# Trainium2 trunk step: window attention moved from a stage of its own into the delta-rule steps

## The chip, the cores and the metric

The kernel runs on one core of one Trainium2 chip. The metric is the device time of one execution in microseconds. A core has engines with instruction queues of their own: TensorE (PE, its weight loads shown as PEld), VectorE (DVE), ScalarE (ACT), GpSimd (POOL) and SyncE (SP), which here issues all transfers. They wait for one another by semaphores.

## The reference, cut to what matters

Two layers are run over 128 prompt tokens and 512 sample tokens. The change concerns the mixer of the even layer, which has two halves side by side behind one input projection:

```
qa, ka, va, qkv_b, gate_b, ab = split(h @ w_in)
# half A: softmax attention, 8 heads of 64, 2 key heads, a sink logit for each head
prompt: oa = softmax_sink(qa ka^T / 8) va                      # 128 queries, 128 keys
sample: qa, ka = rope(qa), rope(ka)
        for each of 4 tiles of 128 queries: keys = 128 cached + the tile and its two neighbours, |q - k| <= 128
# half B: gated delta rule, 4 heads of 128, forwards and backwards over the tiles, a state carried along
for each chunk: A = strict(K K^T * decay * beta);  R = (I + A)^-1
        v_new = R (beta v - beta decay K S);  o = (q decay) S + (QK^T * decay) v_new;  S = decay S + K^T v_new
ob = rmsnorm(o_fwd + o_bwd, out_norm) * silu(gate_b)
out = concat(oa, ob) @ w_out
```

The adaLN modulation of both layers, silu(c) @ w_mod, reads a matrix of 1024 x 12288 floats and is needed in pieces from the even layer's output on.

## The kernel before, in words

Activations lie with features on partitions and 640 token columns (TW) side by side: tile 0 is the prompt, tiles 1 to 4 the sample. Matrix products with large weights are made from three products of rounded halves (hi and lo): `hi` on ACT makes the high part, `w_rest` on DVE the low one. Everything runs in the order in which each engine's part of the program is written; nothing is scheduled at run time.

The even layer has these stages. First the input projection, 23 blocks of 128 columns (`proj`); the last four of them, E_GATE and on, are the gate blocks, and keys and values of half B are turned to token rows between them (`kv_turn`, copied out of PSUM by `k_rows` on ACT and on DVE). Then five delta steps, `for r in range(NT)`: step r handles one tile in each direction (c = 0 forwards, c = 1 backwards; the fifth handles the prompt both ways). In a step the triangular inverse is built in levels: at each level PE makes a product into the z part of a bank (`crossed_mm`, L2418), DVE masks it (`level_z`, L1705), PE makes two products of it (L2471, L2474), and DVE adds them (`r_blocks`, `t_blocks`, L1711, L1714). After the levels come the solve (L2528), the decay rows of the next step (`gc_rows`, L2372) and output and state (L2542, L2543, L2545).

In the gaps of each step PE makes 8 pieces of the modulation product, each with 1 MB of w_mod (`mod_piece`, `mod_first_half`, L2212, L2221). SP loads the pieces two halves ahead into MSLOTS = 4 buffers, a buffer being free when `mod_done` says that its piece is used. Each step also rotates one block of queries or keys of half A (`rope_swap_a`, L2364, and three DVE operations).

After the delta steps comes the attention stage: 40 units (tile, head) in the order of ALLU. For a unit PE makes scores (`att_scores`, L2577, two heads in one call), DVE adds the mask and takes the row maximum (L1806), ACT takes the exponential with its sum (L1095) and that of the sink (L1097), PE turns the probabilities (`att_turn`, L2202), ACT copies them (L500), PE multiplies with the values (`att_values`, L2600), and DVE scales by the reciprocal sum (L1791). The norm and gate of half B (`on_step`) are spread over the same units, and `keep_busy` products (L2207) stand between them. Then `out_halves(0)` begins the output projection (L2081) with blocks m = 0 and 1, and ACT's `out_proj(0)` splits the weights from m = 2 on (L1115).

Of the kernel before, what the change touches and what calls it, by code (L numbers as in the profile page):

```python
# [109 lines left out]
def build(nc, a, outs):  # L110
# [21 lines left out]
    NORMS = (("first", KD, 1), ("l2", 8, 8), ("on", 4, 8), ("cq", C_Q // P, 1), ("ckv", C_KV // P, 1))  # L132
# [162 lines left out]
    MSLOTS = 4  # L295
# [3 lines left out]
    MROW = place("mod_rows", [512], R_T + 4 * al(TW))  # L299
    SM = [place(f"scores{s}", [512], R_F + 1024 + 512 * s) for s in range(2)]  # L300
    PR = [place(f"probs{s}", [512], R_F + 2048 + 512 * s) for s in range(2)]
    PT = [place(f"probs_t{s}", [512], R_F + 3072 + 512 * s) for s in range(2)]
    ASM = place("attn_small", [256], R_F + 4096)
    OA = [place(f"o_attn{s}", [512], R_F + 512 * s) for s in range(2)]
# [154 lines left out]
    ALLU = [(t, c + 4 * g2) for t in ATT for c in range(4) for g2 in range(2)]  # L459
    A_ROPE = (4, 0, 1, 2, 3)  # L460
    ON_AT = [4 + 8 * h for h in range(B_HEADS)]

    def on_head(u, step):

        return ON_AT.index(u - step) if u - step in ON_AT else None

# [25 lines left out]

    def att_copy_a(act, u):

        t, h = ALLU[u]
        c0, c1 = att_local(t)
        act.wait_ge(S("a_turned"), u + 1)
        if u >= 2:
            act.wait_ge(S("a_pv"), u - 1)
        act.activation(PT[u % 2][:, c0:c1], PS[:, 1024 + 512 * (u % 2) + c0:1024 + 512 * (u % 2) + c1], ACT.Copy  # L500
                       ).then_inc(S("a_pt"), 1)


# [60 lines left out]
    with stack:  # L564
# [4 lines left out]
        def _(sp):  # L569
# [43 lines left out]
            for n in range(23):  # L613
                if n < E_AB:
                    load(n, ein_v[:, :, (6 + n) * P:(7 + n) * P])
                elif n == E_AB:
                    load(n, ein_v[:, :, 22 * P:22 * P + 16])
                    sp.dma_start(CT[:, C_FOUR, 0:16], consts[:, C_FOUR, 0:16]).then_inc(S("consts_landed"), 16)
# [3 lines left out]
                elif n < E_QA + 4:  # L622
                    load_two(n, [ein_v[:, :, 64 * h:64 * h + 64] for h in (n - E_QA, n - E_QA + 4)])
                else:
                    c = n - E_QA if n < E_GATE else n - 1
                    load(n, ein_v[:, :, c * P:(c + 1) * P])
            sp.dma_start(CT[:, C_AMASK:, :], consts[:, C_AMASK:, :]).then_inc(S("consts_landed"), 16)
# [130 lines left out]
        def _(act):  # L758
# [238 lines left out]

            for r in range(NT):
                for c in range(2):
# [6 lines left out]
                    act.activation(DQ[c][:, :, :], DQ[c][:, :, :], ACT.Exp, scale=-1.0).then_inc(S("d_exp"), 1)  # L1006
                for c in range(2):
# [43 lines left out]
            o_copy(NT - 1, 0)  # L1051


            def on_step(u):

                h = on_head(u, 0)
                if h is not None:
                    if h == 0:
                        for c in range(2):
                            act.wait_ge(*both("o_done", c, NT))  # L1060
                    if h >= 2:
                        act.wait_ge(*of("stat", "on", 2 * (h - 1)))
                    act.activation(ONSQ[h % 2][:, :], OD[:, h, :], ACT.Square).then_inc(S("norm_sq"), 1)
                for hf in range(2):
                    cs = slice(hf * HW, hf * HW + HW)
                    h = on_head(u, 2 + 2 * hf)
# [21 lines left out]
            for u, (t, h) in enumerate(ALLU):  # L1088
# [10 lines left out]
                if u >= 1:  # L1099
                    att_copy_a(act, u - 1)  # L1100
# [1734 lines left out]
```

## Time and profile before

| what | value |
|---|---|
| runs | 1902.68 us median of 3 (1900.95 to 1903.35) |
| the profiled execution | 1901.23 us, of which the span from first to last instruction is 1899.4 us |
| PE, PEld busy | 1808.8 us (95%), 1667.0 us (88%) |
| DVE, ACT, POOL busy | 988.6, 816.0, 55.8 us |
| TensorE clock granted, mean | 0.997 of full speed |
| the five delta steps | 221.5 to 434.2 us of the span |
| the attention stage | 434.2 to 529.6 us |

A matmul's busy time counts from its start to its modelled end, so a row of n matmuls is shorter than n times their mean: they overlap. A float matrix product in 32 bits stands in the trace as two records, a turn by transposition as one.

### The profile page before, as it was taken

The page shows a single profiled execution, that of the slowest core. Times are in us where ns is not written, and L with a number is a line of the kernel's source. Part 1 is how long each engine was busy: PE and PEld are TensorE (multiplying, and loading weights), DVE is VectorE, ACT ScalarE, POOL GpSimd, SP SyncE. Part 2 cuts the span into 40 slices and gives each one's busy share as a digit, 9 for nine tenths or more (in the row PEclk, how much of TensorE's full clock was granted, in tenths as well). Part 3 has the DMA queues.
Part 4 walks back from the last instruction along what each step waited for, and adds up shares of the span by engine and source line. Part 5 has one row for each costly group of instructions (what it writes and reads, how often), then busy time and mean ns, then how long its engine had stood idle before and what let it go on. Part 6 is the DMA issues. An engine that isn't in the chain of part 4 may idle for free. (4 is left out here: it accounts for less than half of the span.)

```text
span 1899.4 us, 36570 instructions
## 1 busy us (share of the span) xinstructions
PE 1808.8 (95%) x14803; PEld 1667.0 (88%) x14803; DVE 988.6 (52%) x1838; ACT 816.0 (43%) x1396; POOL 55.8 (3%) x57
## 2 busy tenths in 40 slices
PE   5999989988899999999999999999999999999998
PEld 3999867667799999999999887776899999999997
DVE  4443345656747655235556843344376553355555
ACT  4545422225745544124445654343455442243453
POOL 0000222220000000000000000000000000000000
PEclk9999999999999999999999999999999999999999
DMA  7232376751021222222234311011211232122243
GB/s 289 67 69 57 122 222 214 214 178 57 1 72 45 78 74 86 72 67 74 70 99 140 94 49 31 24 33 31 67 45 56 77 89 78 56 77 77 81 135 117
DMA packets 244627, 170.25 MB, mean 90 GB/s; under 512 B 20922, under 2 KB 231068, under 8 KB 243356
## 3 DMA queue, kind: packets, MB, share of 16 engines
q1 hardware_dynamic: 244508, 168.55, 29.8%
q8 instruction: 88, 1.44, 0.3%
q14 instruction: 31, 0.25, 0.0%
HBM read 165.09 MB, written 3.44 MB: 89 GB/s over the span
## 5 line engine op out<-in xcount | busy, mean ns | idle before, releaser
L769 ACT ACTIVATE w_hi<-w_raw 128x1024 fp32r<-128x1024 f32 (+4 forms) x186 | 197.7, 1063 | 529.2 <-PE ps L2003 416.1
L1351 DVE TENSOR_TENSOR w_lo<-w_raw,w_hi 128x1024 fp32r<-128x1024 f32 (+4 forms) x190 | 233.0, 1227 | 346.9 <-ACT w_hi L769 346.5
L2003 PE MATMUL ps<-h_hi,w_hi 128*128 128x320 f32 x1632 | 373.9, 310 | 4.4 <-ACT conv L1178 2.4
L2003 PE MATMUL ps<-h_hi,w_lo 128*128 128x320 f32 x1632 | 371.8, 309 | 0.0
L2003 PE MATMUL ps<-h_lo,w_hi 128*128 128x320 f32 x1632 | 371.7, 309 | 0.0
L2003 PEld LDWEIGHTS ps<-h_hi,w_hi 128*128 128x128 f32 x1632 | 272.8, 188 | 6.5 <-ACT conv L1178 2.9
L2003 PEld LDWEIGHTS ps<-h_lo,w_hi 128*128 128x128 f32 x1632 | 273.0, 188 | 0.0
L2003 PEld LDWEIGHTS ps<-h_hi,w_lo 128*128 128x128 f32 x1632 | 272.8, 188 | 0.0
L2081 PE MATMUL ps<-g_hi,w_hi 128*128 128x320 f32 x352 | 110.1, 313 | 3.2 <-DVE g_lo L1850 2.0
L2081 PE MATMUL ps<-g_lo,w_hi 128*128 128x320 f32 x352 | 108.8, 309 | 0.0
L2081 PE MATMUL ps<-g_hi,w_lo 128*128 128x320 f32 x352 | 108.8, 309 | 0.0
L1357 DVE SCALAR_TENSOR_TENSOR conv<-u,vec_cols,conv 128x511 f32<-128x511 f32 x200 | 101.3, 548 | 14.4 <-ACT conv L1178 11.6
L1361 DVE SCALAR_TENSOR_TENSOR conv<-u,vec_cols,conv 128x511 f32<-128x511 f32 x200 | 100.7, 546 | 0.0
L2081 PE MATMUL ps<-h_hi,w_out_hi 128*128 128x320 f32 x288 | 90.4, 314 | 0.1
L2081 PE MATMUL ps<-h_hi,w_out_lo 128*128 128x320 f32 x288 | 89.0, 309 | 0.0
L2081 PE MATMUL ps<-h_lo,w_out_hi 128*128 128x320 f32 x288 | 89.0, 309 | 0.0
L1183 ACT ACTIVATE g_hi<-gated 128x640 f32 (+1 forms) x44 | 32.6, 742 | 105.1 <-DVE gated L1848 105.1
L2081 PEld LDWEIGHTS ps<-g_hi,w_hi 128*128 128x128 f32 x352 | 66.1, 188 | 4.5 <-DVE g_lo L1850 2.5
L1178 ACT ACTIVATE conv<-ps,vec_cols 128x640 f32<-128x640 f32 x88 | 69.3, 787 | 0.0
L2081 PEld LDWEIGHTS ps<-g_lo,w_hi 128*128 128x128 f32 x352 | 66.1, 188 | 0.2
L2081 PEld LDWEIGHTS ps<-g_hi,w_lo 128*128 128x128 f32 x352 | 66.1, 188 | 0.0
L1868 DVE COPY f_t<-ps 128x640 f32 (+1 forms) x16 | 13.2, 825 | 98.3 <-PE ps L2003 80.5
(364 smaller groups left out, 3299.6 us busy)
## 6 DMA issues: line engine op xcount, KB each, us to landing
w_raw<-in_ffn_w_up SPq DMA_DIRECT2D x88, 512.0 KB, 3.8
w_mod_raw<-in_w_mod SPq DMA_DIRECT2D x80, 512.0 KB, 4.5
w_raw<-in_ffn_w_down SPq DMA_DIRECT2D x48, 704.0 KB, 4.6
w_raw<-in_ev_w_in SPq DMA_DIRECT2D x18, 512.0 KB, 3.8
w_mod_first<-in_w_mod SPq DMA_DIRECT2D x8, 1024.0 KB, 15.8
w_raw<-in_ev_w_out SPq DMA_DIRECT2D x8, 512.0 KB, 4.7
w_raw<-in_od_w_out SPq DMA_DIRECT2D x8, 512.0 KB, 4.1
w_raw<-in_od_w_kv_up SPq DMA_DIRECT2D x24, 128.0 KB, 2.3
```

Source lines behind the costliest of these rows:

```text
L769: act.activation(WH[slot][:, 0:k, :], RAW[slot][:, 0:k, :], ACT.Copy).then_inc(w_hi, 1)
L1178: act.activation(halves(Y[b][:, :]), pair(b0 + 2 * slot), ACT.Copy, scale=vcol(v0 + b * FCH, j)).then_inc(evac_a, 1)
L1183: act.activation(row(Gh, j), GP[:, :], ACT.Copy).then_inc(S("g_hi_written"), 1)
L1351: dve.tensor_tensor(WL[slot][:, 0:k, :], RAW[slot][:, 0:k, :], WH[slot][:, 0:k, :].bitcast(F32), ALU.subtract).then_inc(w_lo, 1)
L1357: dve.scalar_tensor_tensor(y[:, c0 + 1:c1], u[:, c0:c1 - 1], w_before, y[:, c0 + 1:c1], ALU.mult, ALU.add).then_inc(S(signal), 1)
L1361: dve.scalar_tensor_tensor(y[:, c0:c1 - 1], u[:, c0 + 1:c1], w_after, y[:, c0:c1 - 1], ALU.mult, ALU.add).then_inc(S(signal), 1)
L1868: dve.tensor_copy(halves(row(F, m)), pair(2 * slot)).then_inc(evac_v, 1)
L2003: last = pe.matmul(out, w_of(k, wi), x_of(k, xi, i), start=(k == 0 and p == 0), stop=(k == ks - 1 and p == 2))
L2081: last = pe.matmul(out, w[wi][:, k, :], x[xi][:, k, tk(g)], start=(k == 0 and p == 0), stop=(k == ks - 1 and p == 2))
```

## The change

- The attention stage goes. Step r of the delta loop now carries all heads of one tile (r = 0 the prompt, r = 1 to 4 the sample tiles 1 to 4). The two heads c and c + 4, which have different key heads, form a pair. Scores of pair q are made at level q (0 to 3), its maxima on DVE at level q + 1, its two turns at level q + 2 and its values at level q + 3, the last of them in the final level. The scores lie in banks 2 and 5, the values in the upper half of banks 1 and 4, and the products of the levels move to the banks that are left.
- In the prompt's step all eight heads are one batch: scores at level 1, maxima at level 2, turns at levels 3 and 4, values at level 5.
- The sink's exponential and the division are made once a step for eight heads (`sink_args`, `att_sink`, `normalise`); the result is turned at the start of the next step and copied into the place of the queries.
- The rope products go to the gate blocks (E_GATE - 1 to 22), one after each, on bank 7, so `kv_turn` has three banks (4, 5, 6) in turn where it had four.
- MSLOTS falls from 4 to 3; the tables for mask, cosine and sine are loaded earlier.
- Within a step k_times_state moves from levels 4 and 5 to levels 0 and 1, and piece 6 of the modulation from level 5 to the final one.
- Norm and gate of half B and the split of half A follow as a tail (`on_square` ... `on_rest`), 640 columns at a time; `first_chunks` multiplies each 128 rows of the activations with output blocks 0 and 1 as they come. The `keep_busy` products of this place go.

```diff
-    MSLOTS = 4
+    MSLOTS = 3
-    A_ROPE = (4, 0, 1, 2, 3)
+    A_ROPE = (0, 1, 2, 3, 4)
+    S_BANK, O_BANK, O_AT = (2, 5), (1, 4), 128
+    TAIL = (0, 1, 2, 4, 3, 5, 6, 7)
@@ ScalarE
-                act.activation(KTOK[:, t, :, :], q4(bank(4 + 2 * (t % 2))), ACT.Copy).then_inc(S("k_tok"), 1)
+                act.activation(KTOK[:, t, :, :], q4(bank(4 + (2 * t) % 3)), ACT.Copy).then_inc(S("k_tok"), 1)
...
+                att_exps(r, 0)
+                for q in range(pairs(r)):
+                    att_pt_copy(r, q, 0)
+                    if q + 1 < pairs(r):
+                        att_exps(r, q + 1)
+                    else:
+                        att_sink(r)
+                    att_pt_copy(r, q, 1)
...
-            for u, (t, h) in enumerate(ALLU):
...
+            on_square(0)
+            att_hi(0)
+            hi(N0_EVEN_OUT)
+            on_square(1)
+            on_root(0)
...
+            on_out(3)
-            act.wait_ge(S("on_lo"), B_HEADS)
+            act.wait_ge(S("on_lo"), 4 + B_HEADS)
             out_proj(0)
@@ VectorE, after the masks level_z of a level
+                    if r == 0:
+                        if lv == 1:
+                            sink_scaled()
+                        elif lv == 2:
+                            prompt_max()
+                        elif lv == 3:
+                            sink_args(0)
+                    elif lv < 5:
+                        pair_max(r, lv - 1)
+                    else:
+                        sink_args(r)
...
+                normalise(r)
                 for c in range(2):
                     dve.wait_ge(*both("v_solved", c, r + 1))
@@ TensorE
             def kv_turn(t):
-                for kind, sem in ((1, "k_tok"), (2, "v_tok")):
-                    if t >= 2:
-                        pe.wait_ge(S(sem), t - 1)
+                for kind in (1, 2):
+                    x = 2 * t + kind - 1
+                    if x >= 3:
+                        pe.wait_ge(S(("v_tok", "k_tok")[kind - 1]), (x - 3) // 2 + 1)
...
+                if n >= E_GATE - 1:
+                    rope_swap_a(n - E_GATE + 1)
...
+                if r > 0:
+                    att_out_turn(r - 1)
...
+                        if lv < 4:
+                            mod_first_half(r, lv + 2)
+                        if lv == 1 and r < NT - 1:
+                            k_times_state(r, 1)
+                        if lv > 2:
+                            for c in range(2):
+                                pe.wait_ge(*both("t_written", c, t0 + lv))
+                            att_values(r, lv - 3)
+                        if lv > 1:
+                            att_turn(r, lv - 2, 0)
...
+                        if lv < 4:
+                            mod_piece(r, lv + 2, halved=True)
+                        if lv > 1:
+                            att_turn(r, lv - 2, 1)
+                        if lv < 4:
+                            att_scores(r, lv)
...
                 if r < NT - 1:
+                    pe.wait_ge(S("oa_scaled"), r + 1)
                     gc_rows(r + 1)
...
-            pe.wait_ge(S("a_rotated"), NT)
-            keep_busy(7, 3)
...
+            att_out_turn(NT - 1)
+            mod_turn(MROUNDS + 1, MROW, 6)
...
+            out_halves(0, on_stat)
```

On TensorE, the third step's (r = 2) level 3 before: the two products of z, half a piece of the modulation, the product for level 3 of both directions, the other half (names as in the code; the rows of 64 x 32 products repeat).

```order
L2418 MATMUL ps<-r_blocks_176,a_blocks_178 64x64 x8
L2418 MATMUL ps<-r_blocks_177,a_blocks_179 64x64 x8
L2221 MATMUL ps<-w_mod_raw_190,silu_c 32x256 x4
L2471 MATMUL ps<-level_z_170,t_blocks_172 64x32 x2
L2474 MATMUL ps<-t_blocks_172,level_z_170 64x32 x2
...
L2221 MATMUL ps<-w_mod_raw_190,silu_c 32x256 x4
```

The same place now:

```order
L2589 MATMUL ps<-r_blocks_176,a_blocks_178 64x64 x8
L2589 MATMUL ps<-r_blocks_177,a_blocks_179 64x64 x8
L2330 MATMUL ps<-w_mod_raw_189,silu_c 32x256 x4
L2547 MATMUL ps<-v_attn_tok,probs_t 128x64 x8
L2311 MATMUL ps<-consts,probs_193 128x128 x4
L2660 MATMUL ps<-level_z_170,t_blocks_172 64x32 x2
L2663 MATMUL ps<-t_blocks_172,level_z_170 64x32 x2
...
L2330 MATMUL ps<-w_mod_raw_189,silu_c 32x256 x4
L2311 MATMUL ps<-consts,probs_193 128x128 x4
L2517 MATMUL ps<-qa_ka_va 128x128 x4
L2517 MATMUL ps<-k_ctx_cols,qa_ka_va 128x128 x2
L2517 MATMUL ps<-qa_ka_va 128x128 x2
```

The values of pair 0 and the first turn of pair 1 stand between the z products and the level's own, and the second turn and the scores of pair 3 behind them.

On VectorE, level 2 of the same step now; before, the two masks were followed at once by the four additions.

```order
L1813 TENSOR_TENSOR level_z_170<-ps,consts 128x256
L1813 TENSOR_TENSOR level_z_171<-ps,consts 128x256
L1739 ISA probs_193,attn_small<-ps,consts,sink_scaled 128x512
L1739 ISA attn_small 128x1
L1739 ISA probs_193,attn_small<-ps,consts,sink_scaled 128x512
L1739 ISA attn_small 128x1
L1713 TENSOR_SCALAR attn_small<-attn_small 128x2
L1833 TENSOR_TENSOR r_blocks_176<-r_blocks_176,ps 128x32x4
L1836 TENSOR_TENSOR t_blocks_172<-t_blocks_172,ps 128x32x4
L1833 TENSOR_TENSOR r_blocks_177<-r_blocks_177,ps 128x32x4
L1836 TENSOR_TENSOR t_blocks_173<-t_blocks_173,ps 128x32x4
```

The mask and maximum of a pair stand between the masks of z and the additions that wait for the level's products.

On ScalarE, the head of the tail, behind the last copy of the delta output; before, these stood among the exponentials of the units.

```order
L1001 ACTIVATE qa_ka_va<-ps 128x4x128
L1107 ACTIVATE on_sq_205<-o_delta 128x640
L1112 ACTIVATE h_hi<-qa_ka_va 128x640
L769 ACTIVATE w_hi_58<-w_raw_56 128x1024
L1107 ACTIVATE on_sq_206<-o_delta 128x640
L1119 ACTIVATE on_rstd_207<-ps,eps 128x640
L1122 ACTIVATE on_rstd_207<-on_rstd_207 128x640
L769 ACTIVATE w_hi_57<-w_raw_55 128x1024
```

They are whole rows of 640 columns in a fixed order, 20 of them and two weight blocks.

## Rows read from the trace of the kernel before

**Rows 1.** Windows by stage: length, busy of each engine, clock, DMA share, GB/s.

```profile
219.40:270.00 50.60, 43.14 (x819) 32.87 (x819) 24.35 (x70) 15.03 (x34) 11.85 (x12) 0.93 0.73 223
315.00:357.00 42.00, 38.75 (x811) 29.73 (x811) 25.75 (x79) 11.68 (x30) 10.91 (x10) 1.00 0.67 207
436.00:482.00 46.00, 40.19 (x355) 33.26 (x355) 31.40 (x124) 32.36 (x89) 0.00 (x0) 1.00 0.10 30
```

**Rows 2.** Timeline of DVE: each step's first operation, and the last state.

```profile
221.51 1.49 DVE L1672 TENSOR_TENSOR d_qk<-ps,decay_sum 128x512 f32<-128x512 f32 x2 [8.41 <-PE ps L2372]
...
268.39 0.69 DVE L1672 TENSOR_TENSOR d_qk<-ps,decay_sum 128x512 f32<-128x512 f32 x1 [3.64 <-PE ps L2545]
...
312.87 0.69 DVE L1672 TENSOR_TENSOR d_qk<-ps,decay_sum 128x512 f32<-128x512 f32 x1 [2.45 <-PE ps L2545]
...
352.33 0.69 DVE L1672 TENSOR_TENSOR d_qk<-ps,decay_sum 128x512 f32<-128x512 f32 x1 [2.45 <-PE ps L2545]
...
395.29 0.69 DVE L1672 TENSOR_TENSOR d_qk<-ps,decay_sum 128x512 f32<-128x512 f32 x1 [2.45 <-PE ps L2545]
...
434.44 0.69 DVE L1748 COPY state<-ps 128x512 f32<-128x512 f32 x1 [1.04 <-PE ps L2545]
```

**Rows 3.** Timeline of one pair: scores, next work, a turn, values, mask and exponential.

```profile
456.27 0.75 DVE L1806 CUSTOM_DVE_ANT_0 scores<-ps,consts,sink_scaled 128x512 f32<-128x512 f32 x1
457.29 0.71 ACT L1095 ACTIVATE probs<-scores,attn_small 128x512 f32<-128x512 f32 x1
457.84 0.71 PE L2577 MATMUL ps<-qa_ka_va 64*128 64x128 f32 x8
458.93 0.66 PE L2202 MATMUL ps<-consts,probs 128*128 128x128 f32 x4
459.31 0.97 PEld L2600 LDWEIGHTS ps<-v_attn_tok,probs_t 128*128 128x128 f32 x8
```

**Rows 4.** Groups of the window 315:357: count, busy, mean, idle before and releasers.

```profile
L2471 PEld LDWEIGHTS ps<-level_z,t_blocks 64*64 64x64 f32 x160 | 5.1, 134 | 1.5 <-DVE level_z L1705 1.2
L2418 PEld LDWEIGHTS ps<-r_blocks,a_blocks 64*64 64x64 f32 x160 | 5.1, 134 | 2.3 <-DVE r_blocks L1711 1.2 <-issue 0.8 <-DVE r_blocks L1699 0.2
...
L2510 PEld LDWEIGHTS ps<-level_z,t_blocks 64*64 64x64 f32 x16 | 0.6, 134 | 1.3 <-DVE level_z L1732 1.3
```

**Rows 5.** Windows of 3 us after a wait for w_mod, as in rows 1.

```profile
237.00:240.00 3.00, 0.35 (x4) 0.23 (x8) 0.36 (x1) 0.00 (x0) 0.00 (x0) 0.77 0.47 156
240.00:243.00 3.00, 3.00 (x80) 2.00 (x72) 0.82 (x4) 0.00 (x0) 0.00 (x0) 0.50 0.75 221
243.00:246.00 3.00, 3.00 (x48) 1.94 (x40) 1.00 (x3) 0.00 (x0) 0.00 (x0) 0.59 0.81 264
```

**Rows 6.** Timeline of PE: a wait inside one group of products.

```profile
284.99 0.24 PE L2471 MATMUL ps<-level_z,t_blocks 64*64 64x32 f32 x1 [2.15 <-issue]
```

**Rows 7.** Transfers of w_mod in 318:335, from issue to landing.

```profile
DMA to landing us min/median/max: 3.9/4.4/5.0
```

**Rows 8.** Timeline after the first gate block: turns on PE, then ACT.

```profile
193.76 1.91 PE L2202 MATMUL ps<-consts,qkv_b 128*128 128x128 f32 x16
...
197.01 1.08 ACT L945 ACTIVATE k_tok<-ps 128x512 f32<-128x512 f32 x2
```

**Rows 9.** Groups of 433:530 that the tail keeps, as in rows 4.

```profile
L1063 ACT ACTIVATE on_sq<-o_delta 128x640 f32<-128x640 f32 x4 | 2.9, 723 | 0.0
L769 ACT ACTIVATE w_hi<-w_raw 128x1024 fp32r<-128x1024 f32 x2 | 2.1, 1046 | 0.0
L1763 DVE TENSOR_TENSOR o_delta<-o_delta,silu_gate 128x640 f32<-128x640 f32 x4 | 3.3, 818 | 0.0
```

**Rows 10.** Timeline: table load and weights on ACT and DVE, first product of block m = 2.

```profile
528.78 1.28 ACT L1126 ACT_TABLE_LOAD   x1
...
531.17 2.36 DVE L1464 TENSOR_TENSOR w_out_lo<-w_raw,w_out_hi 128x1024 fp32r<-128x1024 f32 x2 [1.68 <-ACT w_out_hi L1115]
...
536.70 0.31 PE L2081 MATMUL ps<-h_hi,w_out_hi 128*128 128x320 f32 x1
```

More of the change, by code:

```diff
@@ L298, in build @@
     MPARTS = KD * MROUNDS
[L299 to L304, printed above, removed]
+    MROW = place("mod_rows", [512], R_G + 5 * TW)
+    SM = [place(f"probs{s}", [2, 512], R_RAW + MSLOTS * 2 * D + 1024 * s) for s in range(2)]
+    ASM = place("attn_small", [256], R_RAW + MSLOTS * 2 * D + 2048)
+    assert MSLOTS * 2 * D + 2304 <= 6 * KMAX * P
+    PT = place("probs_t", [2, 512], R_T + 2176)
+    OA = place("o_attn", [512], R_A + (NT + 3) * P + 16)
     KW = PAST + TW
@@ new lines, in on_out @@
+            def on_out(h):
+                act.wait_ge(S("on_gated"), 2 * h + 2)
+                act.activation(Hh[:, 4 + h, :], OD[:, h, :], ACT.Copy).then_inc(S("on_hi"), 1)
+            for c in range(2):
+                act.wait_ge(*both("os_done", c, NT))
+            on_square(0)
[3 more added lines that the diff above has]
+            on_root(0)
+            hi(N0_EVEN_OUT + 1)
+            att_hi(1)
+            on_square(2)
+            on_root(1)
+            att_hi(2)
@@ L1111, in out_split @@
+            on_square(3)
+            on_out(0)
+            att_hi(3)
+            on_root(2)
+            on_out(1)
+            on_root(3)
+            on_out(2)
+            on_out(3)
             def out_split(n0, m):
@@ L1773, in rope @@
+            mod_out(MROUNDS - 1, 6)
+            att_lo(0)
+            w_rest(N0_EVEN_OUT)
+            on_gate(0)
+            w_rest(N0_EVEN_OUT + 1)
+            att_lo(1)
+            att_lo(2)
+            on_gate(1)
+            on_rest(0)
+            att_lo(3)
+            on_gate(2)
+            on_rest(1)
+            on_gate(3)
+            on_rest(2)
+            on_rest(3)
+            for i in range(4, 8):
+                gains(i // 4, i // 2 % 2, 1 + i % 2)
             def rope(dst, b, turned, n):
@@ new lines, in att_turn @@
+            def att_turn(r, q, g2):
+                p = batch(r, q)
+                pe.wait_ge(S("a_exp"), p + 1)
+                if q or g2:
+                    pe.wait_ge(S("a_pt"), 2 * p + g2)
+                elif r == 0:
+                    pe.wait_ge(S("k_out_rows"), 1)
+                elif r < NT - 1:
+                    pe.wait_ge(*both("v_minus", 1, r + 1))
+                else:
+                    pe.wait_ge(S("mod_cols"), r + 1)
+                for c0 in [P * c for c in range(4)] if r == 0 else [c0 for c0, kt in att_tiles(r)]:
+                    last = turn(PS[:, 7 * 512 + c0:7 * 512 + c0 + P], SM[p % 2][:, g2, c0:c0 + P])
+                last.then_inc(S("a_turned"), 1)
@@ new lines, in att_values @@
+            def att_values(r, q):
+                p = batch(r, q)
+                pe.wait_ge(S("a_pt"), 2 * p + 2)
+                if r == 0:
+                    pe.wait_ge(S("v_rows"), 2)
+                for c in range(4) if r == 0 else (q,):
+                    for g2 in range(2):
+                        o0 = 512 * O_BANK[g2] + O_AT + 64 * c
+                        tiles = [(P * c, 0)] if r == 0 else att_tiles(r)
+                        for x, (c0, kt) in enumerate(tiles):
+                            last = pe.matmul(PS[:, o0:o0 + 64], PT[:, g2, c0:c0 + P], AV[:, kt, 64 * g2:64 * g2 + 64],
+                                             start=(x == 0), stop=(x == len(tiles) - 1))
+                last.then_inc(S("a_pv"), 1)
@@ L2389, in _, with att_out_turn @@
+            def att_out_turn(t):
+                pe.wait_ge(S("oa_scaled"), t + 1)
+                for k in range(4):
+                    last = turn(hb(7, k), OA[:, P * k:P * k + P])
+                last.then_inc(S("oa_turned"), 1)
             gc_rows(0)
```

551 lines of the change are left out of this document (265 added, 286 removed).

## Prediction

> **What bounds the kernel now.** I read the windows by stage first, to see which engine fills which stage. In the delta steps [rows 1] PE is busy 43.14 of 50.6 us in the first step and 38.75 of 42 in the third, while DVE has 24 to 26 us and ACT 12 to 15; the transfers of w_mod move 207 to 223 GB/s. In the first half of the attention stage PE shows 40.19 of 46 us, but there dummy products are counted, and DVE (31.40) and ACT (32.36) work on small pieces. Nobody is full there: the stage is a round of short waits between three engines. It lasts from 434.2 (last product of state; the copy of it starts at 434.44 [rows 2]) to 529.6 us, about 95 us for 40 units, while in the delta steps DVE and ACT lie idle half the time or more. The question is how much of PE's real attention work fits into PE's gaps in the steps, since PE is the engine that the steps already fill.
>
> Then the timeline of DVE for the length of each step [rows 2]: from first operation to first operation 46.9, 44.5, 39.5, 43.0 and, to the last product at 434.2, 38.9 us. The third (r = 2) has no long wait in it, so it is my pattern step.
>
> Then the timeline of a pair [rows 3], for what PE must do. The scores of two heads over 4 key tiles begin at 457.84 and the next work at 458.93: 1.09 us. A turn of 4 tiles begins at 458.93 and the values at 459.31: with its end effects 0.42. Values of one head: 8 weight loads in 0.97, whose last runs 0.1 into the next work: 0.89. A pair is 1.09 + 2 x 0.42 + 2 x 0.89 = 3.7 us. Three key tiles (sample tiles 1 and 4) cost three quarters of it, 0.87 + 0.70 + 1.34 = 2.9. The prompt has one key tile for each head, 3.6 us in all. That is 3.6 + 11.6 + 14.8 + 14.8 + 11.6 = 56.4 us of PE, against the stage's 95.
>
> **The steps (r = 0 to 4), +37.0 us.** In the pattern step the gaps in front of the levels' loads are 1.5, 2.3 and 1.3 us [rows 4], of which 0.8 is "issue", for which no releaser is shown and which I don't count as fillable. Some 4.3 us of gaps are thus covered when other products stand there: the code order puts 0.42 to 3.3 us between a level's product and the next z product. At level 5 only one turn (0.42) stands there, hence a small rest. Step 2 adds 14.8 of pair work and loses a rope product of about 0.45: 14.8 - 0.45 - 4.3 = 10.1. The level with values, scores and two turns (level 3) becomes about 6.7 us, levels 2, 4 and 5 4.7 to 4.9, against 3.3 to 4.3 now.
>
> Is DVE or ACT in the way? At each level DVE makes two masks (0.75), then the pair's maxima, 2 x 0.75 (457-wide row of L1806 [rows 3]) and a negation, about 1.65, and then four additions (0.9): 3.3 us, and once 1.1 more for v_minus. PE needs 4.7 or more. The additions wait for the level's products, which PE now reaches 2 to 3 us after z; pair_max is over by then (0.2 late at level 1 at most). ACT makes two exponentials with sums (0.71 + the read, 0.8 each) and two copies of 0.58: 2.8 us a level. The longest thread, maxima at level q + 1, exponential 1.6 us, turn at level q + 2, has a level's time. `normalise` takes about 1.35 us on DVE in front of v_new; it runs while PE does the solve and the decay rows (1.8 us each), which v_new is waited for after. Cost 0; without that cover it would be 0.5 to 1.3 us a step.
>
> Step 3 like step 2 and 0.5 for scores that wait for o_add on banks 2 and 5: +10.6. Steps 1 and 4 with three key tiles: 11.6 - 0.45 - 4.3 = 6.9, and step 4 again 0.5: +7.4. Step 0: its two waits for w_mod pieces, one before the window at 237 [rows 5], can take up the prompt's scores (1.0); turns and values add 0.8 + 1.8, the rope product goes with 0.5: about +2. Sum 2.0 + 6.9 + 10.1 + 10.6 + 7.4 = 37.0. Bounds: the steps' gaps all fill and the prompt hides: 30; nothing fills: 56.4 - 2.2 = 54, of which I take 37 since the gaps are real and the code order covers them.
>
> Three buffers for w_mod. A half lands 3.9 to 5.0 us after issue [rows 7], and a part (two halves, issued together when a buffer comes free) is there about 5.1 us later, the next ones every 4.3. At a step's start parts 0 to 2 are in the three buffers. Part 3 is issued when part 0 is used, and needed after parts 1 and 2 (1.8), level 0 (0.9), k_times_state (0.9), scores (1.1) and z (1.15): 6.3 us later with the turn of the row. It arrives with about 1 us to spare. Each later part has a level of 4.9 us against 4.3. So cost 0; if every first part were late by 1 us, 4.
>
> **The gate blocks, +4.8 us.** This stage is PE from end to end, so what is put in counts. Four rope products (the fifth hides behind the last silu) of 0.43: 1.7. After the first gate block the fourth turn (x = 3) waits for ACT's first k_tok, since three banks are left for four turns. PE's turns begin at 193.76 [rows 8]; now rope 0.43, three turns of 0.42, so the fourth is asked for at 195.5, but k_tok starts at 197.01 and its first half is there at 197.6 [rows 8], behind the silu and its table load: 2.2 us of wait. After the second block the same with no table load: 0.7. Together 4.6 and the ends of the waits, 4.8. Bounds 1.7 (no wait) and 6.5.
>
> **The tail, -75.5 us.** T is the end of the last step (434.2). Now block m = 2 of the output projection starts at 536.70 [rows 10]: T + 102.5. In the new order ACT's chain rules first: OD complete at T + 1.8, then in order 20 operations of 640 columns, 0.72 each alone [rows 9] and about 0.67 in a row, two weight blocks of 1.05 [rows 9] and about 2 us of waits for DVE: T + 17.7. The last head is gated on DVE (2 x 0.8 [rows 9]) after its root (T + 16.4) and after the third head's work, T + 18.8; its copy on ACT to 19.5, its rest on DVE to T + 20.4. Blocks 0 and 1, which cost 7 us of PE before, are multiplied meanwhile; PE ends them about T + 21.4. But out_proj on ACT starts only at T + 20.4, with the table load 1.28 [rows 10], the split of m = 2 1.05 and its rest on DVE 1.2 [rows 10]: block 2 starts at T + 24. Behind it m = 4 waits for the buffer of m = 2, 1.2 + 1.05 and a landing of 4.5 later, T + 31, just when PE wants it. So -78.5.
>
> TensorE's clock in the tail: in the first step PE was nearly idle (0.35 of 3 us) and the clock fell from 2.4 to 1.2 GHz, and it stood at 0.50 and 0.59 for the next 6 us of full work [rows 5]. In the tail PE has some 3 us of idle before the second weight block, and no keep_busy products. I take one fall with the same loss, 6 x 0.45 = 3 us (the fall at r = 0 stays as it is): -78.5 + 3 = -75.5. Bounds: 0 and two falls, 6. The Trainium skill, page "TensorE: Matmul & The Clock Gate", section "HAM oscillation — how this bites in real kernels", says that PE kept waiting between short bursts is put back to half rate each time. The trace agrees for one wait and not for the shorter one at 231 us, after which the clock was 1.00; by the page the tail could fall twice and the sum be 3 us higher, which is a rival below.
>
> **Sum.** 37.0 + 4.8 - 75.5 = -33.7. The profiled execution took 1901.23 us, its span 1899.4; so span 1865.7, execution 1867.5. It lies 1.45 below the median of the three runs, 1902.68; from the median 1869.0. I say 1868.
>
> **The rivals.**
> The long waits go (0.12). Step 1 is 5 us and step 3 3.5 us longer than step 2; there is a wait of 2.15 us in the middle of a group of products, with no releaser [rows 6], and the clock then falls. Half of these lie near waits for w_mod or heavy transfers. If more work between the levels thins them out and the fall at r = 0 goes (3 us): 1868 - 12 = 1856. For it: the transfers now finish early in each step. Against: the program is as long and PE fetches as many instructions.
> Pairs fit badly (0.12). In-order queues turn into waits: DVE's pair_max in front of the additions, ACT's copy of the second turn behind the next pair's exponentials (it ends within 0.2 us of when the values of level 5 want it), parts of w_mod late. With 1 us at each of 20 levels: 1888.
> The clock falls more often (0.07): as the page has it in the tail, and at the waits of rows 8 and the first step: two falls of 3: 1874, or within my range.
> The pair's chain doesn't ride but stands in the level (0.03): maxima 1.65, exponential 1.6, two turns, two copies and values, 0.84 + 1.16 + 1.78, 7 us for each of 16 levels: steps +116, so 1902.7 + 116 + 4.8 - 75.5 = 1948, slower than before. It decides where a level grows by over (75.5 - 4.8) / 16 = 4.4 us; mine grow by about 2.5. Against it: each part of the chain has its own level in the order of PE.
> The forecast as it stands: 0.66.
>
> **How the numbers follow.** The likeliest is 1868, its own range 1860 to 1878. For 8 in 10 the range takes in the rival below (1856, and 6 less if the gate blocks' waits don't come) and all but the end of the badly fitting case: 1850 to 1888. About 0.2% (4 us) is what a measurement can tell from no change. Faster 0.95, within 0.02 (a badly fitting case at twice its price), slower 0.03.
>
> **What would show it.** Right: the third step lasts about 50 us, all five 250 (now 212.7), with PE near full and no wait of DVE above 1 us at levels 2 to 5; block 2 of the output projection starts 24 to 28 us after the last product of state; a wait of about 2 us of PE on k_tok at 194 us. Wrong: PE idle in front of L2311 or L2547 at each level, waits for w_mod at level 1, a tail above 32 us, or steps of under 46 us, which would say that PE's pitch for the pairs was smaller than in the old stage.

## The result, and the profile after

The changed kernel takes 1870.08 us (median of 4 runs, 1868.44 to 1873.32), the kernel before 1901.82 us (4 runs, 1898.68 to 1903.35). The ratio is 0.9834, with a 95% interval of 0.982 to 0.9849. The profiled execution took 1870.07 us with a span of 1868.3 us, against 1901.23 and 1899.4 before.

First the windows of the five delta steps, of the kernel before and of the changed one, cut at DVE's first operation of each step ([rows 2] gives those of before) and at the copy of the last state. The columns are as in [rows 1].

```profile
221.51:268.39 46.88, 40.26 (x795) 29.96 (x795) 22.74 (x65) 11.66 (x30) 10.87 (x10) 0.93 0.75 228
268.39:312.87 44.48, 40.32 (x817) 31.18 (x816) 23.89 (x74) 12.15 (x30) 10.91 (x10) 0.96 0.73 225
312.87:352.33 39.46, 37.20 (x800) 28.36 (x800) 23.75 (x72) 10.98 (x27) 10.91 (x10) 1.00 0.67 211
352.33:395.29 42.96, 37.86 (x801) 28.48 (x800) 25.02 (x74) 9.86 (x25) 10.89 (x10) 1.00 0.68 212
395.29:434.44 39.15, 34.84 (x775) 25.79 (x774) 24.05 (x68) 10.45 (x26) 10.91 (x10) 1.00 0.51 154
```

```profile
227.76:275.04 47.28, 42.55 (x833) 32.56 (x833) 25.85 (x74) 15.86 (x49) 11.32 (x10) 0.96 0.73 225
275.04:326.04 51.00, 50.31 (x923) 40.49 (x922) 29.01 (x94) 21.40 (x56) 10.90 (x10) 1.00 0.61 196
326.04:378.70 52.66, 52.08 (x947) 42.26 (x946) 29.38 (x94) 21.84 (x53) 10.90 (x10) 1.00 0.51 161
378.70:431.54 52.84, 52.25 (x947) 42.38 (x946) 31.80 (x99) 20.72 (x51) 10.91 (x10) 1.00 0.52 162
431.54:478.93 47.39, 45.61 (x882) 35.90 (x881) 29.34 (x90) 19.72 (x52) 10.91 (x10) 1.00 0.45 139
```

Length less PE's busy time is PE's idle time. The steps together grew from 212.9 to 251.2 us, by 38.2. PE's busy time grew by 52.3 us, from 190.5 to 242.8, and its idle time fell from 22.4 to 8.4. By steps the growth is 0.4, 6.5, 13.2, 9.9 and 8.2 us. In steps 1 to 3 PE is idle for only 0.6 to 0.7 us of 51 to 53. (This is one execution. In two others of the changed kernel, shown below, the steps sum to 253.0 and 252.1 us.)

The timeline of PE in the gate blocks, the rope products (L2392) and the turns (L2311), beside which [rows 8] stands. Ahead of them is one product of the decay rows that both kernels make before any rope product, first of the kernel before and then of the changed one:

```profile
186.06 0.29 PE L2305 MATMUL ps<-log_decay,consts 128*128 128x20 f32 x2
...
186.72 0.29 PE L2425 MATMUL ps<-log_decay,consts 128*128 128x20 f32 x2
...
195.29 1.02 PE L2392 MATMUL ps<-qa_ka_va,consts 128*128 128x512 f32 x2
196.15 1.47 PE L2311 MATMUL ps<-consts,qkv_b 128*128 128x128 f32 x12
199.18 0.66 PE L2311 MATMUL ps<-consts,qkv_b 128*128 128x128 f32 x4 [1.56 <-ACT k_tok L945]
...
206.72 1.02 PE L2392 MATMUL ps<-qa_ka_va,consts 128*128 128x512 f32 x2
207.57 2.27 PE L2311 MATMUL ps<-consts,qkv_b 128*128 128x128 f32 x16
```

One rope product is two records, and it takes 0.86 us, from 195.29 to 196.15. Behind it stands the wait for k_tok. The first step starts 6.25 us later than before, but 0.66 of these are there already at 186.06 and 186.72, ahead of what the change put in. From that product to the first step it is 35.45 us before and 41.04 now, 5.6 more.

The timeline of the tail, from the copy of the last state to block m = 2 of the output projection, with only the rows before which PE waited, the table load, and the marker behind the first half of the projection (the product of the squares of x; of its x12, the first start counts):

```profile
478.93 0.69 DVE L1866 COPY state<-ps 128x512 f32<-128x512 f32 x1 [1.10 <-PE ps L2740]
481.21 1.31 PE L2111 MATMUL ps<-on_sq,consts 128*128 128x320 f32 x4 [1.44 <-ACT on_sq L1107]
487.68 0.42 PE L2168 MATMUL ps<-h_hi,w_hi 128*128 128x320 f32 x1 [2.58 <-DVE w_lo L1390]
498.41 0.41 PE L2168 MATMUL ps<-h_hi,w_hi 128*128 128x320 f32 x1 [1.37 <-DVE h_lo L1887]
499.27 1.28 ACT L1165 ACT_TABLE_LOAD   x1 [0.88 <-DVE h_lo L1887]
503.60 0.60 PE L2168 MATMUL ps<-h_hi,w_out_hi 128*128 128x320 f32 x1 [3.15 <-ACT f_t L813]
```

```profile
L2152 PE MATMUL ps<-x_sq,consts x12: 430/432/537, 544.2 to 1363.0; 128*128 128x320 f32 x12
```

Block 2 starts 24.7 us after the copy of the last state, where it was 102.3 us before [rows 2, 10]: 77.6 us less. The marker is at 544.2, where it was at 575.6 before: 65.3 us after that copy against 141.2, or 75.9 us less. Thus 1.7 us were lost between block 2 and the marker, and the windows of 3 us show where:

```profile
487.00:490.00 3.00, 2.29 (x11) 1.83 (x12) 2.34 (x4) 2.97 (x5) 0.00 (x0) 0.90 0.35 105
490.00:493.00 3.00, 3.00 (x11) 2.41 (x10) 2.94 (x4) 2.08 (x4) 0.00 (x0) 0.53 0.24 72
...
502.00:505.00 3.00, 1.40 (x5) 1.43 (x6) 2.32 (x3) 1.46 (x4) 0.00 (x0) 0.67 0.30 91
505.00:508.00 3.00, 3.00 (x18) 3.00 (x17) 0.23 (x1) 1.32 (x3) 0.00 (x0) 0.76 0.85 249
```

The granted clock fell twice from 2.4 towards 1.2 GHz, each time behind a wait (2.58 and 3.15 us). The second fall slowed products of blocks 2 and 3, on which the end depends: from block 2 to the marker it is 40.6 us here and 40.5 and 40.6 in two other executions, and 38.9 in the kernel before at full clock.

The first fall is not free either. ACT's chain, which sets the tail, waits in it for PE's product of squares:

```profile
491.76 0.80 ACT L1119 ACTIVATE on_rstd<-ps,eps 128x640 f32<-128x640 f32 x1 [0.89 <-PE ps L2111]
```

ACT's copy of the last head starts 18.7 us after the copy of the state. In the run with dummy products below, where the clock stays full there and ACT has no such wait, it is 18.1: the first fall cost this execution 0.6 us.

The three terms are +6.25 for the gate blocks (the first step starts at 227.76, before at 221.51), +38.2 for the steps and -75.9 for the tail. That is -31.4 us, and the span fell by 31.1.

### The profile page after: what moved, and what is told of

It is laid out like the page before. It is cut to its first block and busy times, and to the rows that moved or that the text cites. A ratio compares the mean times of both kernels' runs of the same rounds, so it can differ in the third digit from the quotient of the medians.

```text
span 1868.3 us, 36045 instructions
## 1 busy us (share of the span) xinstructions
PE 1792.6 (96%) x14703; PEld 1657.9 (89%) x14703; DVE 972.7 (52%) x1706; ACT 811.6 (43%) x1351; POOL 56.2 (3%) x57
## 5 line engine op out<-in xcount | busy, mean ns | idle before, releaser
L1955 DVE COPY f_t<-ps 128x640 f32 (+1 forms) x16 | 13.2, 825 | 98.3 <-PE ps L2090 80.6
```

Source lines behind the costliest of these rows:

```text
L1955: dve.tensor_copy(halves(row(F, m)), pair(2 * slot)).then_inc(evac_v, 1)
```

## The experiments

Each run was timed beside the kernel before, whose medians were 1899.7 to 1901.0 us. One execution's profile is good to about 2 us in the steps: waits for w_mod and stalls fall differently in each. Hence I give the medians, and beside them the stages that repeat.

**Three buffers alone.** In the kernel before, one line:

```
-    MSLOTS = 4
+    MSLOTS = 3
```

> The kernel before with three buffers for w_mod instead of four, nothing else. Theory A (the prediction's: the third buffer is enough): 1902 within 2 us, since a half lands 3.9 to 5.0 us after its issue and a level of the delta steps lasts about as long. Rival (three buffers are too few for the short levels of the kernel before, 3.3 to 4.3 us each): PE waits for w_mod at most levels of steps 0 to 4, 0.5 to 1 us each, 1912 to 1920. Second question: do the four waits marked issue inside groups of products (2.15 us at 284.99, 1.02 at 376.77, 1.22 at 382.73, 0.96 at 413.04) stay? If they belong to the length of the program or to its place in memory they stay or move; if they belong to the transfers of w_mod their times change with the buffers.

Measured: 1909.24 us (8 runs), ratio 1.0054 (1.0034 to 1.0074), some 10 us slower. The waits for w_mod are there, here in the timeline of PE in step 2, where the kernel before has none:

```profile
324.72 0.64 PE L2221 MATMUL ps<-w_mod_raw,silu_c 128*32 128x256 f32 x8 [1.44 <-DMA w_mod_raw<-in_w_mod]
329.80 0.64 PE L2221 MATMUL ps<-w_mod_raw,silu_c 128*32 128x256 f32 x8 [1.73 <-DMA w_mod_raw<-in_w_mod]
```

So the prediction's zero is no property of three buffers, as theory A had it, but of the longer levels: the changed kernel has waits for w_mod in step 0 only. (No run has the changed kernel with four buffers.) The four waits marked issue were gone too; 0.79 and 0.70 us at other places stood instead.

**Keys first.** In the gate blocks of the changed kernel, the two copies of k_tok on ACT go ahead of the silu:

```
                 b = 2 * (n % 2)
+                if n >= E_GATE:
+                    for t in range(2 * (n - E_GATE), min(2 * (n - E_GATE) + 2, NT)):
+                        k_rows(t)
...
-                if n >= E_GATE:
-                    for t in range(2 * (n - E_GATE), min(2 * (n - E_GATE) + 2, NT)):
-                        k_rows(t)
```

> The changed kernel with the two copies k_tok ahead of the silu (and its table load) of the same gate block on ACT. Theory A (the wait of PE in front of the fourth turn, 1.56 us at 199.18, is ACT's order): the wait goes to under 0.3 us, 1870.1 - 1.5 = 1868.6, with a second small gain of 0.3 at 208; first delta step starts at about 226.0 instead of 227.76. Rival (the time goes to another wait, since the silu now ends later and the next gate block waits for its banks): no difference, 1870.

Measured: 1871.76 us (1868.24 to 1872.91), no difference to 1870.08. The wait is gone and the first step starts 3.2 us earlier:

```profile
224.55 1.49 DVE L1775 TENSOR_TENSOR d_qk<-ps,decay_sum 128x512 f32<-128x512 f32 x2 [0.46 <-PE ps L2483]
```

Only 2.1 us of that are the edit's. The product of the decay rows, ahead of the gate blocks, stands at 185.61 here and at 186.72 in the changed kernel's first profile; from it to the first step it is 38.94 us instead of 41.04.

The profiled execution lost the gain again, 2.8 us in step 1 (a stall of 0.87 us marked issue among other delays) and 1.1 in the tail, where the second fall of the clock lasted longer. Neither has to do with the edit as far as the trace shows. Five runs are too few to see 2 us through that.

**Early split.** Block 2's weights get a place that is free earlier (the norm buffers move away from it), and the repeated table load goes:

```
             on_root(3)
+            out_split(N0_OUT[0], 2)
             on_out(2)
             on_out(3)
+            act.wait_ge(S("on_lo"), 4 + B_HEADS - 2)
+            out_split(N0_OUT[0], 3)
...
-                act.preload_act_table_set("natural_log_exp_and_others")
-                out_split(n0, 2)
-                out_split(n0, 3)
+                if i:
+                    act.preload_act_table_set("natural_log_exp_and_others")
+                    out_split(n0, 2)
+                    out_split(n0, 3)
```

> The changed kernel with the weights of output blocks 2 and 3 split before the last head is done (block 2's split needs a free place, so the two norm buffers move and the six places are numbered anew), and without the repeated table load. Theory A (of the 3.15 us that PE waits in front of block 2 at 503.60, all but the evacuation of block 0, about 1.2 us, is this split; and the clock's fall behind it costs 1.7 us): block 2 starts 2.0 us earlier, at T + 23, and if the fall goes too the kernel is at 1870.1 - 3.7 = 1866.4. Rival (the wait moves to ACT's chain ahead of it, as one more operation stands in front of the copy of the third head): 1869 to 1870.

Measured: 1869.89 us (1865.24 to 1870.23), again no difference in the median. Its trace: the copy of the last state at 479.96, block 2 at 503.30, 23.3 us later (24.7 without the edit), and the wait in front of it is now 0.45 us:

```profile
499.69 0.41 PE L2177 MATMUL ps<-h_hi,w_hi 128*128 128x320 f32 x1 [1.24 <-DVE h_lo L1894]
503.30 0.53 PE L2177 MATMUL ps<-h_hi,w_out_hi 128*128 128x320 f32 x1 [0.45 <-ACT f_t L813]
```

The marker comes 63.0 us after the copy of the state instead of 65.3. The clock still falls (0.56 in 501:504), now behind the waits for the last heads. So 2.3 us of the 3.7 came, or 1.6 against the shortest tail of the changed kernel's three executions (64.6).

**Dummy products.** In the two long waits of the tail:

```
                         if k == 0:
+                            if m:
+                                keep_busy(3, 5)
...
                     first_chunks(between)
+                    keep_busy(3, 6)
```

> The changed kernel with dummy products on PE in its two waits of the tail (five of 256 columns, 2.1 us, ahead of the second weight block, where it waits 2.58 us, and six, 2.6 us, ahead of block 2, where it waits 3.15 us). Theory A (the clock falls from 2.4 to 1.2 GHz because of these two waits; the first fall costs nothing, since ACT's chain rules, the second costs 1.7 us): granted clock 1.00 from 478 to 511, 1870.1 - 1.7 = 1868.4. Rival (the fall has another cause, or it costs nothing): same clock rows, 1870. If the dummies are too long for the waits, up to 0.5 us is lost.

Measured: 1871.12 us (1869.6 to 1874.91). The first fall is gone, since 484:496 is granted in full, but the clock falls later instead, behind waits of 1.07 and 1.24 us for the last two heads:

```profile
484.00:490.00 6.00, 4.79 (x22) 3.35 (x21) 5.06 (x6) 5.94 (x9) 0.00 (x0) 1.00 0.29 87
490.00:496.00 6.00, 5.97 (x34) 5.02 (x34) 5.27 (x8) 5.94 (x10) 0.00 (x0) 1.00 0.31 87
496.00:502.00 6.00, 3.69 (x17) 3.17 (x16) 5.20 (x10) 3.21 (x4) 0.00 (x0) 0.79 0.00 0
502.00:508.00 6.00, 6.00 (x35) 5.69 (x34) 2.60 (x3) 2.90 (x5) 0.00 (x0) 0.93 0.39 114
```

Theory A failed: the second fall does not hang on the 3.15 us wait alone. The marker was 64.6 us after the state's copy, as in one of the changed kernel's later executions (64.6 and 65.3). The six dummies are a second reason: block 2 starts right behind them with no wait left, 24.5 us after the state's copy where a later execution of the changed kernel has 24.1, and block 3 then waits 0.86 us. So this run does not price the second fall by itself.

**One key tile in the values.** The products of the other tiles are left out:

```
-                        tiles = [(P * c, 0)] if r == 0 else att_tiles(r)
+                        tiles = [(P * c, 0)] if r == 0 else att_tiles(r)[:1]
```

> The changed kernel, in which the product of probabilities and values takes one key tile instead of three or four in steps 1 to 4 (the others are left out, so its output is not the reference's). 160 records of 0.115 us (1.84 us for 16 in a pair) leave PE: 18.4 us, and nothing leaves DVE or ACT. Theory A (PE's own work sets the steps): steps 1 to 4 shorten by 17 to 18.4 us, the kernel is at 1852 to 1853. Rival (the pair's chain over DVE and ACT sets the length of a level): under 8 us, 1862 or more.

Measured: 1856.95 us (1854.7 to 1860.67), 13.8 below the changed kernel in the same job (1870.71). Step 2 went from 52.66 to 48.05 us, 4.6 of the 5.5 us taken out, and there are now waits that were none before:

```profile
360.05 0.63 PE L2547 MATMUL ps<-v_attn_tok,probs_t 128*128 128x64 f32 x4 [0.43 <-ACT probs_t L1027]
```

PE's own work sets the steps, as in theory A, but the pair's chain is close behind: with 5 us less a step it begins to show. Neither theory's number was met; theory A's is the nearer.

**More work on DVE.** In `pair_max` of the changed kernel, ahead of the maxima, one more pass for each head:

```
+                    dve.tensor_reduce(ASM[:, col:col + 1], PS[:, 512 * S_BANK[g2] + c0:512 * S_BANK[g2] + c1], AX_X, ALU.max)
```

> The changed kernel with one more pass of DVE over the scores of each head in steps 1 to 4, ahead of the pair's maxima (0.51 us for three key tiles, 0.68 for four; 32 of them, 19 us of DVE, its result unused). Theory A (DVE has room in each level: 3.3 us of some 5): 0 to 2 us slower, 1870 to 1872. Rival (the in-order queue: the additions that PE waits for stand behind it): 1.0 to 1.4 us in each of 16 levels, 1886 to 1889.

Measured: 1873.03 us (1871.96 to 1876.68), 2.3 above 1870.71. Step 2 took 53.25 us, 0.6 more:

```profile
331.19:384.44 53.25, 52.19 (x946) 42.25 (x946) 34.41 (x102) 21.95 (x53) 10.89 (x10) 1.00 0.50 161
```

DVE's 19 us cost 2.3: it has room, and the in-order queue is no bound.

**The changed kernel again**, unchanged, in two later jobs.

> The changed kernel itself once more, for its spread beside the others: 1870 within 1.5 us. Its stages by the profile: gate blocks, steps 2 and 4 and the tail as before to 0.1 us; steps 0, 1 and 3, which hold the waits for w_mod and the waits marked issue, may move by 1 to 2 us.

> The changed kernel itself beside the three others: 1870 to 1871.

Measured: 1870.71 us (1868.7 to 1872.92) and 1871.39 us (1869.32 to 1874.45). The first steps began at 227.20 and 227.31; step 2 lasted 52.66 and 52.65, step 4 47.39 and 47.40, step 3 53.90 and 53.82, step 0 48.04 and 46.91. The marker stood 64.6 and 65.3 us after the state's copy. In the first of them the clock fell elsewhere in the tail: 0.62 in 484:487, behind waits of 1.45 and 0.79 us, and then full from 490 to 505.

**Less traffic, changed kernel and kernel before.** PE's work stays, most of the weights aren't brought:

```
+                    w = D if u < MSLOTS else P
-                    sp.dma_start(MW[u % MSLOTS][:, D * x:D * x + D], wm[l][:, u % KD, m0 + D * x:m0 + D * x + D]
+                    sp.dma_start(MW[u % MSLOTS][:, D * x:D * x + w], wm[l][:, u % KD, m0 + D * x:m0 + D * x + w]
```

> The changed kernel, in which each transfer of w_mod after the first three parts brings an eighth of its columns (the rest of the weights is left out, so its output is not the reference's). PE's work is the same. Theory A (what is left idle in the steps, 4.7 us in step 0, and the stalls marked issue of some executions come from the w_mod traffic): step 0 goes from 47.3 to 43 us, steps 2 and 4 stay at 52.66 and 47.4, step 1 at 51.0, step 3 at 52.7 to 52.8 in each execution, no wait marked issue above 0.45 us, no fall of the clock in step 0 after the first wait; the time is 1870.7 - 5 = 1866. Rival (the stalls come from the length of the program, the traffic does nothing): steps 1 and 3 as they were, 1869 to 1871.

> The kernel before with the same reduction (all parts after the first four bring an eighth of their columns; the rest is left out, so its output is not the reference's). Theory A (the four waits marked issue, 5.35 us, and the falls of the clock behind them are caused by the w_mod traffic): step 0 goes from 46.9 to 41 to 43 us, step 1 from 44.5 to 40, step 3 from 43.0 to 39.5 to 40, step 2 stays at 39.5, step 4 from 39.15 to 38; in all some 13 us, 1900 - 13 = 1887. Then about 9 us of the gaps that the pairs filled in the changed kernel were made by transfers, and not by the chain of the levels. Rival (the stalls belong to the program): only step 0 gains, 1895.

Measured: the changed kernel 1868.67 us (1865.57 to 1870.05), the kernel before 1890.58 us (1888.93 to 1894.78; ratio 0.9952, 0.9935 to 0.997). The windows of the kernel before with little traffic:

```profile
221.46:267.18 45.72, 40.59 (x795) 30.18 (x795) 22.72 (x65) 11.66 (x30) 10.85 (x10) 0.93 0.43 127
267.18:307.73 40.55, 38.55 (x817) 29.96 (x816) 23.81 (x74) 12.14 (x30) 10.93 (x10) 1.00 0.11 29
307.73:346.96 39.23, 36.94 (x801) 28.20 (x800) 23.72 (x73) 10.99 (x27) 10.90 (x10) 1.00 0.11 30
346.96:386.79 39.83, 36.97 (x801) 28.20 (x800) 25.00 (x75) 9.86 (x25) 10.90 (x10) 1.00 0.11 29
386.79:423.90 37.11, 34.31 (x775) 25.50 (x774) 24.03 (x68) 10.45 (x26) 10.91 (x10) 1.00 0.18 49
```

And those of the changed kernel with little traffic:

```profile
226.71:270.82 44.11, 40.77 (x833) 31.55 (x833) 26.27 (x75) 15.86 (x49) 11.32 (x10) 1.00 0.36 108
270.82:321.82 51.00, 50.31 (x923) 40.49 (x922) 29.01 (x95) 21.41 (x56) 10.89 (x10) 1.00 0.08 23
321.82:374.48 52.66, 52.08 (x947) 42.26 (x946) 29.39 (x95) 21.83 (x53) 10.91 (x10) 1.00 0.08 22
374.48:427.21 52.73, 52.14 (x947) 42.28 (x946) 31.77 (x99) 20.72 (x51) 10.91 (x10) 1.00 0.08 23
427.21:474.60 47.39, 45.61 (x882) 35.90 (x881) 29.32 (x90) 19.72 (x52) 10.90 (x10) 1.00 0.15 42
```

In the kernel before, step 1 fell from 44.5 to 40.55, step 3 from 43.0 to 39.8, step 4 from 39.15 to 37.1, as theory A said; step 0 lost only 1.2 us where 4 to 6 were expected, as the waits for its first parts, which were left whole, stayed (1.68 and 2.24 us). The median fell by 10.4 us where 13 were expected. The four waits marked issue are gone. In the changed kernel step 0 moved, from 47.28 to 44.11, and step 3 read 52.73, where the three executions with full traffic have 52.84 to 53.90. The time fell by 2.0 to 2.7 us where 5 were expected; a wait of 2.15 us in step 0 stayed. (The profiled execution, 1865.57, was the fastest of the four.)

**The three edits together**: keys first, early split, and dummy products (five ahead of the second weight block, two ahead of each of the last two heads), measured in two jobs.

> The changed kernel with all three edits: keys ahead of the silu, the early split, and dummy products in the waits of the tail (five ahead of the second weight block, two ahead of each of the last two heads). If they add up: gate stage 3.2 us shorter (seen in the run with the first edit), block 2 at T + 23.5 and no fall of the clock between 478 and 511, 1.5 to 2 us: 1870.1 - 3.2 - 1.4 - 1.7 = 1863.8. Rival (what is won ahead of step 0 is waited for again in steps 0 and 1, as their w_mod parts come at their own pace): 1867.

> The version with all three edits once more, to tell 1864.8 from 1870.7: 1865 within 2 us, that is 0.3% below the changed kernel in the same job, if its first measurement was no accident; 1869 or more otherwise.

Measured: 1864.8 us (1863.78 to 1872.79) and 1864.44 us (1863.38 to 1870.66), against 1870.71 and 1871.39 for the changed kernel in the same jobs: 5.9 and 6.9 us, 0.3 to 0.4%. One of the five runs in each job took longer, 1872.8 and 1870.7. The first of these is the profiled one: step 0 held one stall, and the clock fell behind it:

```profile
250.51 1.08 PE L2343 MATMUL ps<-w_mod_raw,silu_c 128*32 128x256 f32 x7 [1.84 <-issue]
```

In the other profile (span 1862.7) the first step started at 225.22, the granted clock was 1.00 through the tail, and the marker stood 62.0 us after the state's copy. The marker is 2.6 to 3.3 us nearer than in the three profiles of the changed kernel. From the product of the decay rows to the first step it is 38.95 us, 2.1 less, and not the 3.2 that the expectation counted. The two stages thus explain 4.7 to 5.4 of the 5.9 and 6.9 us. This version beats both kernels.

## Why the prediction was right, point by point

The forecast was 1868 us, and 1870.08 were measured. The mechanism held: the attention stage goes, and PE's own work for the pairs sets the steps. That the steps' sum came so near is in part luck, as two errors cancelled in it.

**The steps, +37.0, measured +38.2.** By steps the numbers were near: step 0 +0.4 against +2, as the prompt's work mostly went into idle time of PE (2.3 us more busy in it), step 1 +6.5 (6.9), step 3 +9.9 (10.6), step 4 +8.2 (7.4). But step 2, the pattern step, was 52.7 us instead of 50 and grew by 13.2 instead of 10.1. The step of the argument that failed is "some 4.3 us of gaps are thus covered". The gaps of [rows 4] are those of the weight loader. This is the place in the kernel before, loader and PE:

```profile
326.18 0.64 PE L2221 MATMUL ps<-w_mod_raw,silu_c 128*32 128x256 f32 x8
...
326.75 1.01 PEld L2418 LDWEIGHTS ps<-r_blocks,a_blocks 64*64 64x64 f32 x32 [0.41 <-DVE r_blocks L1711]
```

The loader is shown waiting 0.41 us for DVE while PE was still at the product before, so nothing was lost there. PE itself was idle for only 2.26 us in this step, of which 1.7 were filled. The pair's price was a little low as well. Here is PE's timeline in step 2 of the changed kernel, scores, turn and values, each with the row behind it:

```profile
337.97 0.39 PE L2517 MATMUL ps<-qa_ka_va 64*128 64x128 f32 x4
338.29 1.15 PE L2589 MATMUL ps<-r_blocks,a_blocks 64*64 64x64 f32 x32
...
345.40 0.66 PE L2311 MATMUL ps<-consts,probs 128*128 128x128 f32 x4
345.99 0.25 PE L2660 MATMUL ps<-level_z,t_blocks 64*64 64x32 f32 x2
...
350.95 2.00 PE L2547 MATMUL ps<-v_attn_tok,probs_t 128*128 128x64 f32 x16
352.79 0.61 PE L2311 MATMUL ps<-consts,probs 128*128 128x128 f32 x4
```

The scores (from 337.20) take 1.09 us, as said, and the values of two heads 1.84, but a turn takes 0.59 (345.40 to 345.99) or 0.53 (352.79 to 353.32) and not 0.42: a pair is 4.1 us and not 3.7. The 0.42 came from the same slip: the row of [rows 3] that ends the turn, at 459.31, is the weight loader's, while PE began the values at 459.42. Against that, the rope product that left the step gave back 1.06 us (330.03 to 331.09 before) and not 0.45, as it is two records. PE's busy time in this step grew by 14.9 us, close to the 14.35 of the prediction; with 1.7 us filled that makes 13.2.

The sum came out because steps 1, 3 and 4 held idle time of another kind. Their long stalls and the half clock behind one of them vanished, as the first rival said ("the long waits go"), which I had priced as a case beside the forecast and not as a part of it. With little traffic the step lengths of the kernel before sum to 202.4 us against 212.9, and those of the changed kernel to 247.9 against 251.2. PE's idle time there is 15.1 us before (202.4 less 187.4 busy) and 7.0 after (247.9 less 240.9). So of the 14.1 us of idle time that the change took out, 8.1 are there without traffic too (6.3 of them in steps 1 to 4, some 1.6 a step, and not 4.3); the other 6 were made by the traffic of w_mod.

Step by step this says what the level gaps were worth. With little traffic in both kernels the steps grow by -1.6, 10.5, 13.4, 12.9 and 10.3 us, in all 45.5. In steps 1 to 4 that is 2.3 to 3.6 us a step above the forecast, the gaps that weren't there. The traffic had cost the kernel before 10.5 us in the steps and costs the changed one 3.3, and these 7.2 us brought 45.5 down to 38.2. The prediction had them in its first rival, at 0.12, and not in its sum.

**DVE, ACT and three buffers at cost 0.** Right, by the run with 19 us more on DVE (2.3 us) and by PE's idle time in steps 1 to 3. Pairs that fit badly, the second rival, found no support. For the buffers the number was right, and the comparison that the prediction made, a part's pitch against a level's length, bears it out: the same edit costs the short levels of the kernel before 10 us.

**The gate blocks, +4.8, measured +6.25** (5.7 and 5.8 in the two other profiles). The waits were nearly as said: 1.56 us for 2.2, and about 0.35 in the second block for 0.7. The term that was mis-sized is "four rope products of 0.43: 1.7". They take 0.86 each, 3.4, as each is two records. From the product of the decay rows on, the growth is 5.6 us in all three profiles; the other 0.1 to 0.7 us come from ahead of the gate blocks, where nothing was forecast, and differ from execution to execution.

**The tail, -75.5, measured -75.9.** Block 2 started 24.9 us after the last product (T = 478.7), where T + 24 was worked out, and its wait for the split, the table load and the evacuation was there. Of the clock I had said one fall of 3 us; there were two, of which the first cost 0.6 (it is in the 24.9) and the second 1.7, together 2.3. The Trainium skill, page "TensorE: Matmul & The Clock Gate", section "HAM oscillation — how this bites in real kernels", tells of a kernel in which PE waits some 3 to 5 us for data between short bursts and is put back to half rate at every one. In this tail the trace agrees for the two longest waits, 2.58 and 3.15 us: 0.53 and 0.67 behind them. It was 1.00 throughout in the run with all three edits, in which no wait of the tail behind 485 was above 1.1 us.

**The sum.** -33.7 against -31.1. The three misses are +1.2, +1.4 and -0.4 us, and 0.3 stands outside these stages.

## What to carry to other kernels

Work moved under a stage that one engine fills costs nearly its full time on that engine. To see what is free, take the stage's length less that engine's own busy time, and not the idle time in front of its weight loads. Then ask what makes that idle time: here the gaps that came from transfers went when the steps became longer (in steps 1 to 4), and they brought 6 us where the gaps from level to level and in step 0 brought 8. To see how much is of which kind, run the kernel before with its transfers cut. A shortage of buffers is a matter of the consumer's pace, so it has to be judged with the new pace and not with the old.

## What the runs showed of the hardware

- A product of 512 columns in f32 with 128 rows is two records and takes 0.86 us at the full clock (195.29 to 196.15). The number behind x in a row counts records.
- In the delta steps PE had stalls marked issue inside groups of equal products, of 0.5 to 2.2 us, while w_mod was being moved at some 200 GB/s: four in the kernel before, none to three in the changed kernel and its variants, at other places in each execution, and none above 0.45 us there with the traffic cut. (Two others, 1.44 us at 1106 and 0.98 at 1313, stand in the later layer at the same products in all kernels.) A stall can bring a fall of the clock behind it (0.73 and 0.70 in 285:291 of the kernel before). The Trainium skill, page "Runtime: NRT & Kernel Launch", section "Instruction fetch mechanics", says that the fetch of straight-line code is hidden by the issue rate. If the fetch is what stalls here, beside heavy transfers it is not always hidden; that it is the fetch, no run here shows.
- The clock fell after waits as short as 1.07 and 1.24 us that lay 2.4 us apart (0.57 in 499:502 of the run with dummy products). The same two waits, of the same length and distance, brought no fall in a later execution of the changed kernel (1.00 in 490:505); there it fell earlier, behind waits of 1.45 and 0.79 us, and later behind that of 3.15 (0.53 in 505:508). So the length of a wait alone does not tell whether the clock falls.
